# Alternating three token groups on each weight tile in the projections of a YOCO decoder step

## The reference

```
h += mixer(rmsnorm(h));   h += (silu(gate) * up) @ w_out  with gate, up = rmsnorm(h) @ w_in   # D_FF = 2816
h += (p[l] @ W_pe) * sigmoid(rmsnorm(h) @ W_pg)                                              # PLE_DIM = 256
after layer 0:  K, V = split(rmsnorm_kv(h) @ w_kv);   layer 1:  q = rmsnorm(h) @ w_b_q,  mix = attention @ w_b_o
attention:  log_a = log_sigmoid(z) + (reverse cumulative sum of log_sigmoid(-z));  a = exp(log_a);  o = a @ v
y = rmsnorm_final(h)
```

## Time and profile before

| | |
|---|---|
| median of three runs | 3438.86 us |
| profiled execution, its own time | 3436.98 us |
| span of the profile | 3435.3 us |
| TensorE (PE) busy, matmuls | 3168.9 us, 92%, x24506 |
| weight loads (PEld) | 2990.2 us, 87%, x24506 |
| VectorE (DVE) busy | 1779.4 us, 52% |
| ScalarE (ACT) busy | 741.2 us, 22% |
| GpSimd (POOL) busy | 988.2 us, 29% |

### The profile page before, as it was taken

How to read it: one execution, slowest core, us unless ns; L and a number is a source line. 1 busy time by engine, 2 the same in 40 slices (tenths; PEclk the granted TensorE clock), 3 DMA queues, 4 the chain that set the end, 5 groups by cost and what they waited for, 6 DMA issues and landing times. The chain is left out here.

```text
span 3435.3 us, 59942 instructions
## 1 busy us (share of the span) xinstructions
PE 3168.9 (92%) x24506; PEld 2990.2 (87%) x24506; DVE 1779.4 (52%) x2670; ACT 741.2 (22%) x1267; POOL 988.2 (29%) x642
## 2 busy tenths in 40 slices
PE   6999999979999999998999878878999999999985
PEld 6888888869999999988899745556999999999985
DVE  4655656575444444465613188786154344434565
ACT  3111111121000000021301076666030000000121
POOL 5212222203232333334332313231233232323232
PEclk9999999989999999999999899899999999999997
DMA  3111111101111111111222555555111111111112
GB/s 102 44 45 45 42 47 39 45 26 44 49 43 49 43 49 43 49 54 57 75 93 93 191 180 191 171 196 187 44 44 43 49 43 49 43 49 43 57 54 75
DMA packets 72526, 247.52 MB, mean 72 GB/s; under 512 B 11058, under 2 KB 15154, under 8 KB 71986
## 3 DMA queue, kind: packets, MB, share of 16 engines
q1 hardware_dynamic: 64594, 221.15, 20.0%
q10 hardware_dynamic: 7776, 24.11, 1.9%
HBM read 218.88 MB, written 26.35 MB: 71 GB/s over the span
## 5 line engine op out<-in xcount | busy, mean ns | idle before, releaser
L1486 PE MATMUL psum<-xh,wh 128*128 128x352 f32 x4032 | 1327.6, 329 | 58.1 <-POOL wl L601 44.7
L1490 PE MATMUL psum<-xl,wh 128*128 128x352 f32 x4032 | 1303.6, 323 | 0.0
L1491 PE MATMUL psum<-xh,wl 128*128 128x352 f32 x4032 | 1302.7, 323 | 0.0
L599 POOL CAST wh<-raw 128x1024 fp32r<-128x1024 f32 x236 | 258.9, 1097 | 2028.2 <-PE psum L1486 1060.7
L1486 PEld LDWEIGHTS psum<-xh,wh 128*128 128x128 f32 x4032 | 766.0, 190 | 79.6 <-issue 56.2
L1490 PEld LDWEIGHTS psum<-xl,wh 128*128 128x128 f32 x4032 | 767.6, 190 | 2.1
L1491 PEld LDWEIGHTS psum<-xh,wl 128*128 128x128 f32 x4032 | 764.8, 190 | 0.0
L601 POOL TENSOR_TENSOR wl<-raw,wh 128x1024 fp32r<-128x1024 f32 x236 | 591.9, 2508 | 18.9
L1034 DVE TENSOR_TENSOR h<-h,psum 128x352 f32<-128x352 f32 x672 | 346.9, 520 | 341.6 <-PE psum L1491 341.4
L1486 PE MATMUL psum<-ah,wh 128*128 128x352 f32 x1344 | 446.4, 332 | 54.4 <-DVE h L1034 23.1
L1490 PE MATMUL psum<-al,wh 128*128 128x352 f32 x1344 | 440.7, 328 | 0.0
(11 more groups left out here) (181 smaller groups left out, 2764.7 us busy)
## 6 DMA issues: line engine op xcount, KB each, us to landing
raw<-in_wstream SPq DMA_DIRECT2D x236, 512.0 KB, 3.6
h<-in_kT_cache SPq DMA_DIRECT2D x64, 512.0 KB, 5.1
h<-in_v_cache SPq DMA_DIRECT2D x64, 512.0 KB, 4.8
h<-in_xT SPq DMA_DIRECT2D x3, 1408.0 KB, 10.8
out_kT_out<-work ACTq DMA_DIRECT2D x8, 528.0 KB, 2.7
out_vT_out<-work ACTq DMA_DIRECT2D x8, 528.0 KB, 2.7
qT_scratch<-work ACTq DMA_DIRECT2D x8, 528.0 KB, 2.7
h_scratch<-h SPq DMA_DIRECT2D x1, 4224.0 KB, 14.3
```

The costliest lines, as they stand in the source:

```text
L599: nc.gpsimd.tensor_copy(wh[:, slot, :], raw[:, slot, :]).then_inc(split_hi, 1)
L1486: ins = mm(out, wh[:, slot, ws], mh, start=first, stop=False)
L1490: mm(out, wh[:, slot, ws], ml, start=False, stop=False)
L1491: return mm(out, wl[:, slot, ws], mh, start=False, stop=last)
```

## The change

A new helper `together` replaces the loop over groups around the k tiles. For each weight tile and each of the three partial products it issues one matmul for each of the three groups, in three banks, before it goes on. It is used in `product_x` where neither `order` nor `sums` is given, in `pair` (but for the very last slab of each feed-forward), in the small product of `ple`, and so in K, V, query and output products too. All three banks are taken at the start and all three units end together. The products of the HGRN layer keep their order. In the attention, the two lane multiplications of a step become one instruction over both lanes.

```diff
@@ attention, VectorE
-                    for e in range(LANES):
-                        dve.wait_ge(scan_done, LANES * i + e + 1)
-                        a = weights[:, i % 3, e, 0:s.width]
-                        nc.vector.tensor_tensor(a, a, r[:, e, lo + 1:CHUNK + 1], ALU.mult).then_inc(a_done, 1)
+                    dve.wait_ge(scan_done, LANES * (i + 1))
+                    a = weights[:, i % 3, :, 0:s.width]
+                    nc.vector.tensor_tensor(a, a, r[:, :, lo + 1:CHUNK + 1], ALU.mult).then_inc(a_done, LANES)
@@ TensorE
+            def together(slot, tiles, xs_hi, xs_lo):
+
+                outs = []
+                for t, tile in enumerate(tiles):
+                    ws = slice(tile * P, (tile + 1) * P)
+                    for part in range(3):
+                        w = wl if part == 2 else wh
+                        for g in range(G):
+                            if t == 0 and part == 0:
+                                unit_start(True)
+                                outs.append(banks.next())
+                            x = (xs_lo if part == 1 else xs_hi)[t]
+                            ins = mm(outs[g][:, 0:GW], w[:, slot, ws], x[:, cols(g)], start=t == 0 and part == 0,
+                                     stop=t == len(tiles) - 1 and part == 2)
+                            if fresh[0]:
+                                ins.then_inc(w_used, 1)
+                                fresh[0] = False
+                            if t == len(tiles) - 1 and part == 2:
+                                ins.then_inc(unit_done, 1)
+
             def product_x(ringed=True, order=None, sums=False):
 
                 slot = slab()
+                if order is None and ringed and not sums:
+                    together(slot, range(KT), [xh[:, k, :] for k in range(KT)], [xl[:, k, :] for k in range(KT)])
+                    return
@@ pair (twice; the last slab of a feed-forward keeps unit_pair)
                 for n in range(KT // 2):
-                    for g in range(G):
-                        unit_pair(slot, n, g)
+                    together(slot, (2 * n, 2 * n + 1), a_hi_, a_lo_)
@@ ple
                     slot = slab()
-                    for g in range(G):
-                        unit_start(True)
-                        b = banks.next()
-                        for k in range(PK):
-                            last = exact(b[:, 0:GW], slot, k, ah[:, k, cols(g)], al[:, k, cols(g)], k == 0,
-                                         k == PK - 1)
-                        last.then_inc(unit_done, 1)
+                    together(slot, range(PK), [ah[:, k, :] for k in range(PK)], [al[:, k, :] for k in range(PK)])
```

More of the change, by code:

```diff
@@ L1703, in pair @@
             def pair(last):
+                a_hi_, a_lo_ = [ah[:, e, :] for e in range(2)], [al[:, e, :] for e in range(2)]
                 slot = slab()
                 for n in range(KT // 2):
-                    for g in range(G):
-                        unit_pair(slot, n, g)
+                    together(slot, (2 * n, 2 * n + 1), a_hi_, a_lo_)
                 slot = slab()
```

## The result

The changed kernel takes 3503.53 us in the median (3499.92 to 3505.97) where the kernel before takes 3438.28 (3437.12 to 3443.4). The ratio is 1.0189, with a 95% interval from 1.0175 to 1.0203: slower by 65 us. The forecast was 3473, with 3496 as its upper end. The profiled execution after took 3505.97 us at a span of 3504.2, so 69 us of span are to be found.

A forecast was written before the change was run, and what follows sets the result against it. TensorE's unbroken matmul pace was taken to bound the feed-forward. With pace and attention at 0, 3436.98 us plus 33.4 for seams and 2 for the lower clock gave 3472.4, rounded to 3473; 8-in-10 range 3444 to 3496.

The forecast's parts named there:

- the pace: Time per matmul over 12312 changed matmuls: 0 ns change, bounds -12 ns (-150 us) to +5 ns (+62 us).
- Rival A: The pace gains as part of the time on top of the columns goes: 3399 or 3323 us; chance 0.10.
- rival C: Worse than the sum: alternation opens small holes or brings the lower clock, 3505 us; chance 0.08.
- Seam 1: Output product to second feed-forward: VectorE's chain starts later at unchanged length; cost 7.3 us.
- seam 2: V to queries: VectorE's chain starts later; cost 7.3 us, at least 4.4 if GpSimd's split falls elsewhere.
- Seam 5: Third product behind a norm (both feed-forwards, K): third matmul waits for its bank; 1.6 us each, 4.8 in all.
- Seam 3: First ple to K: group 1's steps come on top of GpSimd's splits; cost 5.5 us, between 4 and 7.5.
- Seam 4: Last up product of each feed-forward: PE waits for three groups' evacuation and multiplication; 1.7 us each, 3.4 in all.
- Seam 7: End: the last small product's first group is ready after 16 matmuls instead of 6; cost 1.6 us.
- Seam 6: Second small product of each ple: ten more matmuls left after the last bank wait; 3.5 us for two.
- Attention: Merged lane multiplication: saved starts against lane 0's later weights; 0 us, from -7 to +8.
- Rival B: The seams are hidden, with VectorE's chains running faster and attention gaining: 3449 us; chance 0.08.

The follow-up runs named there:

- weights_tiled: Changed kernel with weights in the new order but the token groups of the moving operand in the old order; 3463.22 us.
- bank_only: Changed kernel with operands walked in the order of the kernel before, the bank still changing at every matmul; 3477.5 us.
- groups_rotate: Changed kernel with weights in the old order but the moving operand still rotating over the three token groups; 3499.55 us.
- seams_old: Changed kernel with the order of the kernel before at the seams alone, the new order in the steady products; 3462.12 us, ratio 1.0079.
- merge_only: Kernel before with only the one attention multiplication over both lanes; 3437.86 us.
- after_padded: Changed kernel with k tiles of the four operands 4352 bytes apart instead of 4224; 3476.8 us, ratio 1.0112.

## Why the prediction was wrong

**What failed: the pace, "I take 0 ns".** The bounds were -12 and +5 ns, and it was +2.71 ns, 33.4 us. The two arguments for 0 were both right in what they said. The loads stayed one to one and cost nothing (weights_tiled, 159.14), and a changing bank costs nothing (bank_only, 159.14). But the sentence that listed what the change does to the pace, the stationary tile and the bank, left out a third thing: the order in which the moving operand's groups are read. The windows compared in the earlier trace rows could not show it, since both keep one group for many matmuls. The trace had a sign of it, though: from start to start the two differ by 0.46 ns (158.98 and 159.44), which a count of 64 or 65 can't tell, and bank_only shows the same two paces with the banks alternating, so it is not the bank. groups_rotate shows that it is the whole cost. The condition that the prediction named, "The forecast is wrong if the pace moves by 3 ns", all but came. A loss in pace lay inside the bounds, but no rival had it: A has the gain alone. The window has 1238 matmuls, below the 1240 set for rival C, and C's 3505 us are nearly the measured 3503.53, but that is luck. C's mechanism is holes and the lower clock, and in the window the clock is 1.00 and there is no hole.

Small slips of the prediction change nothing: its 158.9 ns, from the window's count, is 159.14 from start to start, 12 ns would be 148 us and A's lowest time 3325, and the median's 1.9 us on top of 3472.4 make 3474.

**What held: the seams.** 33.8 us by the table, 35 by seams_old.

- Seam 1: 7.3 predicted, 8.1 measured, with the chain's length unchanged.
- Seams 2 and K's part of 5: 8.9 predicted and 9.5 measured. The part of seam 2 that GpSimd's splits might have given back was not: eight steps still take 6.93 us. The products behind take 17.5 and 17.1 us, not "about 19".
- Seam 3: 5.5 predicted; between the first matmul of K and the one that waited 8.14 us the changed kernel falls back by 6.0 us. With half of 6, 7.2 predicted and 6.0 measured, so that 3 was a little too small and 6 too large.
- Seam 4: 4.15 us of wait, 4.3 predicted. Seam 5: 1.48 us, 1.6 predicted. In the two feed-forwards together the rest was 8.4, the prediction 6.6. The difference is mostly the lower clock, for which the prediction had 2 us in all: behind the 4.15 us wait in the first feed-forward the next 19 matmuls start 0.29 us apart at a granted clock of 0.50, while at the same place before they start 0.16 us apart.
- Seam 7: 1.6 predicted, and 1.6 measured over the last gate and small product, their pace taken off. Seam 6 was taken too large: in the second ple, at equal clocks, it cost 0.9 of the 1.75. The last bank came free 2.6 us behind the first matmul and not 4.7, so that of the ten more matmuls, 2.9 us at 0.29, two thirds were given back.

**Attention.** 0 predicted, with -7 to +8 around it; -1.1 in the changed kernel, 0 in merge_only. The runs can't say more: the four kernels with two multiplications took 442.1 to 451.6 us here (mean 448.0), the fifteen with one 439.4 to 449.3 (mean 444.8), one execution each. PE now waits less often for the multiplication and longer, as these two rows of its waits over the same part of the program (2001 to 2433 us after) say; the earlier trace rows has those of before, 13 times and 20.8 us.

```profile
PE psum L1796 <- ACT work L958: 43.6, 45, 1.7
PE psum L1796 <- DVE work L1428: 21.4, 8, 4.2
```

**Rival B** (seams hidden) falls, as every seam's wait is in the trace and only seam 6 was partly absorbed. **Rival A** falls for this change: its threshold of 2.9 ns was nearly reached, with the other sign.

## What to carry to other kernels

A reordering of matmuls changes three streams, the stationary tile, the bank and the moving operand; cost each of them, and look for a row where that very stream changes as it will. At a pace of 12312 equal matmuls one nanosecond is 12 us, so a pace taken as "unchanged" needs a range that can hold a few. Completing several units together costs their lead wherever the next norm or product hangs on the first of them, and it can be read beforehand from VectorE's chain: how early it starts before the product's end, and who waits for its last step.

## What the runs showed of the hardware

- With a weight load for each, matmuls of 352 columns ran at 158.3 to 161.9 ns at full clock, with gaps that repeat to a nanosecond. The Trainium skill, "TensorE: Matmul & The Clock Gate", section "Back-to-back issue gap", has N/2.4 + 2.5 ns as the gap of a single matmul without its load; an estimate by it is 149.2 ns for 352 columns, and no run, each with a load per matmul, came near it.
- In the feed-forwards the pattern follows the sequence of the moving operand's starts modulo 256 bytes (010 instead of 010/101 took 1.85 ns off each matmul in after_padded), and neither banks nor weight order nor the weights' place changed it.
- Some sequences have two patterns, and what ran before chooses: remainder 0 alone 160.0 or 161.1, 000111 158.9 or 161.1. Remainder 128 bytes alone was the fastest, at 158.3. Why, and what makes the gaps themselves, stays open. So does whether rows of other widths behave like this.
